# Hybrid sparse/differential attention layers: projection chunks by row block in two banks, and side steps regrouped

## The reference

```python
h = _rmsnorm(x, pre_norm_g[i]); z = h @ w_in[i]
qa, ka, va, qi, ki, wi, ga, qb, kb, vb, gb = _split_in(z)      # rope on q, k of all groups
# group A: an indexer scores the keys, each query keeps its 64 best admissible ones
iscore = sum_h relu(qi_h . ki / 8) * wi_h
oa = softmax(qa . ka / 8 over the kept keys) @ va              # 8 heads of 64
# group B: differential attention, block-causal in chunks of 64
attn = softmax(q1 . k1 / 8) - lam * softmax(q2 . k2 / 8)       # 4 heads, 2 maps each
ob = _rmsnorm(attn @ vb, subln_g[i]) * (1 - lam_init)
y = concat([oa * silu(ga), ob * silu(gb)]) @ w_out[i]
x = x + _rmsnorm(y, post_norm_g[i])
e = (p[i] @ w_ple_proj[i]) * sigmoid(x @ w_ple_gate[i])
x = x + _rmsnorm(e, ple_norm_g[i])
```

## Time and profile before

| | us |
|---|---|
| median of 3 runs | 362.15 (361.76 to 362.46) |
| profiled execution, its own time | 362.61 |
| span of its trace | 360.8 |
| PE busy | 351.3 |
| DVE, ACT, POOL busy | 264.8, 226.9, 68.1 |

### The profile page before, as it was taken

One profiled execution on the slowest core, in us unless ns is written; L12 is line 12 of the kernel. 1 busy time (PEld: TensorE's weight loads), 2 busy tenths in 40 slices (PEclk: granted clock), 3 DMA queues, 4 the chain that ended last, 5 costly groups with the idle time before them and its releaser, 6 DMA issues.

```text
span 360.8 us, 5644 instructions
## 1 busy us (share of the span) xinstructions
PE 351.3 (97%) x1901; PEld 290.0 (80%) x1901; DVE 264.8 (73%) x560; ACT 226.9 (63%) x459; POOL 68.1 (19%) x121
## 2 busy tenths in 40 slices
PE   7999999999999999999999999999999999999992
PEld 6897887888888888888888888778888878888881
DVE  2884977989966676786786587888996658678543
ACT  3985476686678764655665565778576786365221
POOL 1144173061500000003105315004250000000000
PEclk9999999999999999999999999999999999999999
DMA  7994378763764455657575828347458337550011
GB/s 253 380 358 133 105 228 150 258 184 109 201 212 128 161 180 171 184 171 154 187 216 161 255 74 236 109 124 219 127 160 239 127 118 233 173 162 17 0 51 67
DMA packets 31948, 61.12 MB, mean 169 GB/s; under 512 B 2376, under 2 KB 4688, under 8 KB 31920
## 3 DMA queue, kind: packets, MB, share of 16 engines
q1 hardware_dynamic: 30784, 57.48, 50.6%
q0 software_dynamic: 1120, 3.28, 4.5%
q10 hardware_dynamic: 16, 0.00, 0.0%
HBM read 59.71 MB, written 1.05 MB: 168 GB/s over the span
## 4 chain that ended last, share of the span: by engine, by line
PE 92%; issue 2%; DMA 2%; DVE 1%; ACT 1%; SPq 0%; POOL 0%; POOLq 0%; DVEq 0%
PE proj L1157 26%; PE proj L1159 25%; PE proj L1158 25%; PE sc L1298 3%; PE sc L1240 3%; PE tr L1311 2%; DMA resid<-in_x_dram 2%; PE tr L1258 2%; PE pv L1332 2%; PE pv L1327 1%; PE proj L1118 1%; PE proj L1097 1%; PE proj L1109 1%; PE sc L1189 1%; PE sc L1269 0%
## 5 line engine op out<-in xcount | busy, mean ns | idle before, releaser
L1157 PE MATMUL proj<-w_hi,act_hi 128*128 128x512 f32 (+1 forms) x400 | 160.8, 402 | 0.0
L1159 PE MATMUL proj<-w_hi,act_lo 128*128 128x512 f32 (+1 forms) x400 | 155.3, 388 | 0.0
L1158 PE MATMUL proj<-w_lo,act_hi 128*128 128x512 f32 (+1 forms) x400 | 154.9, 387 | 0.0
L798 DVE TENSOR_TENSOR w_lo<-raw,w_hi 128x1024 fp32r<-128x1024 f32 (+1 forms) x102 | 122.0, 1210 | 20.7 <-ACT w_hi L581 19.7
L581 ACT ACTIVATE w_hi<-raw 128x1024 fp32r<-128x1024 f32 (+2 forms) x103 | 103.3, 1025 | 4.5 <-DMA raw<-in_w_ple_proj_dram 2.1
L1159 PEld LDWEIGHTS proj<-w_hi,act_lo 128*128 128x128 f32 x400 | 75.1, 188 | 15.9
L1157 PEld LDWEIGHTS proj<-w_hi,act_hi 128*128 128x128 f32 x400 | 75.2, 188 | 15.4 <-issue 0.7
L1158 PEld LDWEIGHTS proj<-w_lo,act_hi 128*128 128x128 f32 x400 | 75.3, 188 | 13.0
L522 POOL TENSOR_TENSOR rstd<-var,minus_half 128x1 f32<-128x1 f32 x12 | 6.8, 564 | 182.6 <-DVE var L788 160.6
L699 ACT ACTIVATE probs<-probs,neg_max 128x128 f32<-128x128 f32 (+1 forms) x64 | 28.2, 445 | 1.9 <-DVE neg_max L941 1.9
L581 ACT ACTIVATE pT<-tr 128x512 f32<-128x512 f32 (+1 forms) x22 | 12.7, 576 | 16.3 <-PE tr L1311 11.0
(11 more groups left out here) (179 smaller groups left out, 410.4 us busy)
## 6 DMA issues: line engine op xcount, KB each, us to landing
raw<-in_w_in_dram SPq DMA_DIRECT2D x59, 512.0 KB, 4.4
raw<-in_w_out_dram SPq DMA_DIRECT2D x16, 512.0 KB, 3.4
raw<-in_w_ple_gate_dram SPq DMA_DIRECT2D x16, 512.0 KB, 3.9
raw<-in_w_in_dram SPq DMA_DIRECT2D x7, 324.0 KB, 5.0
raw<-in_w_ple_proj_dram SPq DMA_DIRECT2D x4, 512.0 KB, 3.6
resid<-in_x_dram SPq DMA_DIRECT2D x2, 512.0 KB, 8.0
probs<-in_w_in_dram SPq DMA_DIRECT2D x2, 512.0 KB, 9.3
g_ple<-in_ple_norm_g_dram POOLq DMA_DIRECT2D x2, 512.0 KB, 7.1
```

Of the source, the lines that this page charges most:

```text
L798: nc.vector.tensor_tensor(w_lo[:, g % SLOTS, 0:nk * cols], landing(g, nk * cols), w_hi[:, g % SLOTS, 0:nk * cols].bitcast(fp32), ALU.subtr ...
L1157: nc.tensor.matmul(ps, src_hi[:, b, k0 + k, :], hi, start=(first_u and k == 0), stop=False)
L1158: nc.tensor.matmul(ps, src_hi[:, b, k0 + k, :], lo, start=False, stop=False)
L1159: last = nc.tensor.matmul(ps, src_lo[:, b, k0 + k, :], hi, start=False, stop=last_k)
```

## The change

1. The pieces of the middle chunks run by row block: four of block 0, then four of block 1. All chunks but QB now use the banks `proj0` (block 0) and `proj1` (block 1). `wait_bank` is rewritten for it: GA's block b now waits for `glu_done` of GB's block b.
2. S2 is issued right behind S1, at place 15, and S5 right behind S4, at 42, on TensorE alone; they go to `proj2` and `proj3`. VectorE reads them at the old steps S2 (18) and S5 (44).
3. PV3 moves from 43 to 42 and there stands behind the logits; PV4 moves from 50 to 52, ahead of PV5. PT8 goes to `kT` and does not wait for a value product.
4. The sigmoid and product of GB's row block 0 become a step of their own, `glu`, at place 46.
5. Other places: S3, E3 one earlier, S4, E4 one later, PT3 and PT4 one earlier, PT5 and PT6 one later, T KA 0 at 32.

The core of the diff:

```diff
-    KA=[33, 37],
-    S=[12, 15, 18, 35, 41, 43],
-    E=[13, 16, 24, 37, 42, 44],
+    KA=[32, 37],
+    S=[12, 15, 18, 34, 42, 44],
+    E=[13, 16, 24, 36, 43, 44],
-    PT=[19, 23, 26, 41, 42, 44, 45, 50, 51],
-    PV=[20, 25, 28, 43, 50, 52],
+    PT=[19, 23, 26, 40, 41, 45, 46, 50, 51],
+    PV=[20, 25, 28, 42, 52, 52],
+    glu=46,
+S_WITH = {1: 2, 4: 5}
-        mms(chunk, both, dict(enumerate(mid[c * len(both):(c + 1) * len(both)])))
+        mms(chunk, one(0) + one(1), dict(enumerate(mid[c * len(both):(c + 1) * len(both)])))
-            return 2 * (IN_CHUNKS.index(chunk) % 2) + b
+            return 2 + b if chunk == "QB" else b
...
+        def s_bank(i):
+            return proj[2 + i % 2] if i // 2 in S_WITH.values() else sc[i % 2]
+        def pt_slot(n):
+            return kT[:, :, :] if n == 8 else pT[:, n % 3, :, :]
...
+                elif kind == "glu":
+                    wait_sum(act, L, "GB", 0, s[1])
+                    gate_sigmoid(L, "GB", s[1])
...
                 elif chunk == "GA":
-                    pe.wait_ge(v_out, L * 4 + 2 + b + 1)
+                    pe.wait_ge(glu_done, L * 4 + b + 1)
+                elif chunk == "WO" and b == 0:
+                    pe.wait_ge(max_done, L * 12 + 12)
...
-                elif kind == "S":
+                elif kind == "S" and s[1] not in S_WITH.values():
...
+                    logits(L, s[1], g, b, keys)
+                    if s[1] == 1:
+                        pe.wait_ge(z_out, L * 8 + 2)
+                        logits(L, 2, g, b, keys)
+                    elif s[1] == 4:
+                        pe.wait_ge(max_done, L * 12 + 6)
+                        logits(L, 5, g, b, keys)
```

More of the change, by code:

```diff
@@ L594, in emb_copy, with gate_sigmoid @@
                 copy(emb[:, b, n * N:(n + 1) * N], proj[bank_of("PLE", n, b, L)][:, :]).then_inc(ple_out, 1)
+            def gate_sigmoid(L, chunk, b):
+                if chunk == "GA":
+                    act.wait_ge(y_done, L * 2 + b + 1)
+                elif L > 0:
+                    act.wait_ge(t8_done, (L - 1) * 12 + t8_index("y", b, 0) + 1)
+                nc.scalar.activation(gate[:, b, :], proj[bank_of(chunk, 0, b)][:, :], ACT.Sigmoid).then_inc(sig_done, 1)
             act.dma_start(g8[:, :], pre_norm_g[0, :].rearrange("(k p) -> k p", p=P)).then_inc(g8_in, 16)
@@ L633, in _ @@
                     else:
[L634 to L639, removed]
+                        gate_sigmoid(L, chunk, b)
+                elif kind == "glu":
+                    wait_sum(act, L, "GB", 0, s[1])
+                    gate_sigmoid(L, "GB", s[1])
                 elif kind == "pT":
@@ L801, in _ @@
                 kind = s[0]
[L802 to L805, removed]
+                if kind in ("mm", "glu"):
+                    chunk, n = UNITS[s[1]][:2] if kind == "mm" else ("GB", 0)
+                    b = s[-1]
+                    if kind == "mm" and (s[1] != LAST_OF[chunk, n] or chunk not in ("GA", "GB") or (chunk, b) == ("GB", 0)):
                         continue
@@ L1110, in rest_part, with logits @@
                                      w_hi[:, u, k * cols:(k + 1) * cols], start=False, stop=False)
+            def logits(L, n, g, b, keys):
+                for j in range(N // keys):
+                    for part in range(1 if b == 0 else 3):
+                        for odd in range(2):
+                            m = s_task(2 * n + odd)[2][j]
+                            rows = slice(odd * HEAD, (odd + 1) * HEAD)
+                            if b == 0:
+                                q, k = qT[g][rows, m // 2, 0:P], kT[rows, m // 2, :]
+                            else:
+                                q = (q_lo if part == 2 else q_hi)[rows, m // 2, :]
+                                k = (k_lo if part == 1 else k_hi)[rows, m // 2, :]
+                            end = part == (0 if b == 0 else 2)
+                            ins = nc.tensor.matmul(s_bank(2 * n + odd)[:, j * keys:(j + 1) * keys], q, k,
+                                                   start=(part == 0), stop=end)
+                            if end and j == N // keys - 1:
+                                ins.then_inc(s_done, 1)
             def low_part(u, b, src_hi):
@@ L1284, in _ @@
                     else:
[L1285 to L1290, removed]
-                                rows = slice(odd * HEAD, (odd + 1) * HEAD)
-                                if b == 0:
-                                    q, k = qT[g][rows, m // 2, 0:P], kT[rows, m // 2, :]
-                                else:
-                                    q = (q_lo if part == 2 else q_hi)[rows, m // 2, :]
-                                    k = (k_lo if part == 1 else k_hi)[rows, m // 2, :]
-                                end = part == (0 if b == 0 else 2)
-                                ins = nc.tensor.matmul(sc[odd][:, j * keys:(j + 1) * keys], q, k, start=(part == 0),
-                                                       stop=end)
-                                if end and j == n_maps - 1:
-                                    ins.then_inc(s_done, 1)
+                        pe.wait_ge(max_done, L * 12 + {1: 2, 3: 4, 4: 8}[s[1]])
+                    logits(L, s[1], g, b, keys)
[5 more added lines that the diff above has]
+                        logits(L, 5, g, b, keys)
                 elif kind == "PT":
@@ L1326, in _ @@
                         if g == 0:
-                            last = nc.tensor.matmul(pv[:, h * P:(h + 1) * P], pT[:, n % 3, j, :],
+                            last = nc.tensor.matmul(pv[:, h * P:(h + 1) * P], pt_slot(n)[:, j, :],
                                                     v_all[:, kt, 0, h * P:(h + 1) * P], start=(kt == 0),
```

29 lines of the change are left out of this document (14 added, 15 removed).

## The result

The changed kernel takes **366.48 us** (median of 5 runs, 365.40 to 367.18) against 362.15 before (5 runs, 361.76 to 362.46). The ratio is 1.0106, with a 95% interval of 1.0090 to 1.0122: slower by 1.1%. The forecast was 365.8, within 363.5 to 368.5.

A forecast was written before the change was run, and what follows sets the result against it. The prediction took TensorE's queued work as the bound, busy 351.3 of 360.8 us. Per layer +2.44 - 0.44 - 0.17 = +1.83, +3.66 for two, on 362.61 gives 366.27, as a median 365.8 (range 363.5 to 368.5).

The forecast's parts named there:

- The chain to piece 48: From PV3 through ScalarE's exponentials and sigmoid to VectorE's product of GB: GA's first piece starts 2.44 us later per layer.
- the drain of 1.38: At ScalarE's table load before the sigmoid: by the skill page, 1.4 us longer wait per layer, sum 368.6; not adopted.
- Part 1: Logits S1 and S2 in one TensorE visit: 0.44 us saved per layer.
- Part 2: S4, S5 and PV3 in one visit: pieces 40 to 47 take 15.61 against 16.03, 0.42 us saved per layer without waits.
- Part 3: PV4 and PV5 together at place 52: 0.17 us saved per layer.
- behind another one it adds 1.01: Value product directly behind another in one visit: costs 1.01 us, where PV4 alone costs 1.18.
- The restart: TensorE resuming after its waits before GA's first piece: 0.15 us beyond the wait, with 0 and 0.3 as ends.
- The sum: Per layer +2.44 - 0.44 - 0.17 = +1.83 us; +3.66 for two layers.
- The signs: Trace marks expected: two waits per layer, E4 behind qT_a, 24 logits in a row, TensorE busy about 2 us less.
- The wait was there: Rival at GA's first piece: no wait there, so only savings stand, 360.1 us; 11 in 100, partial waits included.
- No further waits: Rival around places 16 to 25: more waits on ScalarE and VectorE, 368.2 us; 11 in 100 for over 1 us.
- The clock did not fall: Rival behind the new wait: TensorE's clock drops to 1.2 GHz for two pieces, 2.7 us per layer, 371.2; 4 in 100.

The follow-up runs named there:

- e1: Changed kernel with GA in banks proj2 and proj3, so its first piece no longer waits for GB's product; 362.46 us, ratio 0.9991.
- e2: Changed kernel with E4 ahead of PV3's copy on ScalarE and S5's maxima one place earlier, at 43; 364.53 us, ratio 1.0046.
- e6: Kernel before, with GA's first matmul of block 0 also waiting for VectorE's product of GB's block 0; 369.83 us, ratio 1.0188.
- e4: Kernel e3 with S2 moved back to place 18 and the sc banks, in a visit of its own; 361.38 us, ratio 0.9968.
- e3: Changed kernel with GA in proj2 and proj3 and E4 ahead of PV3's copy; 359.99 us, ratio 0.9914; repeated on another chip 360.91 us, ratio 0.9949.
- e5: Kernel e4 with PV4 also moved back to place 50; 361.72 us, ratio 0.9992.
- e10: Changed kernel with the transposes PT6 moved from place 46 to 48, behind GA's first piece; 369.43 us, ratio 1.0191.

## Why the prediction was right, and where its terms were off

**The chain to piece 48: right, nearly row by row.** All times of the profile after are 0.21 later (piece 40 starts at 103.48 and not 103.27: an opening 0.70 longer, less 0.48 saved). With that taken off:

| step | predicted | measured, less 0.21 |
|---|---|---|
| PV3 starts | 109.98 | 110.00 |
| its copy `qT_a` | 111.12 | 111.14 |
| E4 starts | 112.54 | 112.58 |
| sigmoid starts | 120.27 | 120.31 |
| product of GB ends | 121.59 | 121.63 |
| piece 48 starts | 121.74 | 121.69 |

The wait came in two parts as worked out, 0.84 and 1.54 for "about 1.0" and "about 1.7". The term was +2.44 per layer and measured +2.38. e1 and e2 show by taking them away that these were its two causes, and e6 that the wait gives the same 18.4 with nothing else changed.

The trace shows no drain around the table load: it starts at 119.23 and lasts 1.28, and the sigmoid starts at 120.52, 0.01 behind. By the drain of 1.38 that the Trainium skill gives (ScalarE: Activation LUTs, "What ACT_TABLE_LOAD costs") the sum was 368.6; the runs gave 366.48, and the measurement decides.

**Part 1 (S1 and S2): right,** 0.44 predicted, 0.48 in the changed kernel, 0.43 to 0.46 by e4.

**Part 2 (S4, S5, PV3): right as to the visit, too large as to the stretch, and without effect on this result.** I worked out 15.61 for pieces 40 to 48 if nobody waits; e3 shows 15.80, so 0.24 saved and not 0.42. The visit behind piece 42 is nearly as predicted: pieces 42 and 43 with it take 4.20 + 1.51 = 5.71 in e3, for 1.37 + 2.85 + 1.37 = 5.59, and 0.09 of the 0.12 is the slower first matmul behind PT4's transposes, which is in their 0.45 already. Most of the 0.19 lies at PT5 and PT6. Pieces 45 to 47 with their two transposing visits take 1.72 + 1.96 + 1.47 = 5.15, for 3 x 1.37 + 2 x 0.45 = 5.01. The transposes of PT6 are the place: `tr` is freed by PT5's copy (115.62, 0.59 long) and they start right behind it.

```profile
115.94 0.40 PE L1193 MATMUL proj<-w_hi,act_lo 128*128 128x512 f32 x1
116.26 0.66 PE L1335 MATMUL tr<-ident,probs 128*128 128x128 f32 x4
```

That is a wait of about 0.1, which stands in no list of waits. In the changed kernel the whole term can't be seen: piece 48 starts when ScalarE's chain ends, whatever TensorE has saved after PV3. I had counted it in the same way ("not 0.42 earlier").

**Part 3 (PV4 and PV5): right in sign, half the size.** 0.17 predicted, 0.33 measured by e5. The failed step is "behind another one it adds 1.01". That figure came from PV3 behind a row of projections and ahead of logits, which is another neighbourhood. Between two value products nothing else stands, as the rows of both show:

```profile
126.42 1.53 PE L1356 MATMUL pv<-pT,v_all 128*64 128x128 f32 x24
127.78 0.61 PE L1356 MATMUL pv<-kT,v_all 128*64 128x128 f32 x8
```

Piece 52 with its side steps lasts 3.87 in e3, for 3.00 before with one product less: the second one costs 0.87. The first one alone costs 1.17 (piece 50 lasts 2.89 with it and 1.72 without), as predicted (1.18). That the difference is the change of form is my reading, here and in Part 1. The runs show what a visit costs alone and behind another; they don't separate the form from the rest of going in and out, and four transposes, whose form is that of the pieces, also make the first matmul behind them 0.09 slower. In the changed kernel 48 to 56 shows only 0.18 less, since piece 48 restarts there 0.13 slower (1.49 for 1.36).

**The restart: 0.15 taken, about 0.2 measured** (0.06 from the end of the product to piece 48, and 0.13 inside it).

**The sum.** +1.83 per layer predicted, +1.72 in the trace. 3.44 for both layers on the median of before gives 365.6, and the median measured is 0.9 above it. In the profiled run 0.70 of that is a longer opening. The other four runs have no trace, so where the 0.9 lies in them stays open; the interval of the ratio, 3.3 to 4.4 us, has room for 3.44.

**The signs.** Most came as written: both waits twice (1.54 and 0.84), E4 behind `qT_a`, 24 logits in a row, 18.4 between pieces 40 and 48, a clock of 1.00 behind the wait. One was wrong: TensorE's busy sum fell by 0.3 and not by about 2. The busy time of the middle pieces fell by 0.68 and 0.64 per layer and not by 1.03: in pieces 40 to 48 it is 16.03 as before, because the modelled ends of the matmuls ahead of the two waits count as busy and hide what Part 2 saved. The opening of the profile has 0.98 us more busy time.

**The rivals.** The wait was there. No further waits came: pieces 0 to 40 are shorter by exactly the saving. The clock did not fall, but here the forecast had luck. I had looked at the length of the parts beside the last idle stretch; e6 and e10 show that an unbroken stretch of 2.2 to 3.1 us can be enough, and that the same kernel without PT6 between its two waits did lose 2.8 us in one layer. 4 in 100 was too little for this rival. The Trainium skill's rule (TensorE: Matmul & The Clock Gate, "Why this matters for your kernels") that gaps without work take the clock down is borne out in layer 0 of e10 and not in its layer 1, behind an equal gap; e6 shows a fall with a gap of 2.19 us, which is shorter than those that the page warns of.

## What to carry to other kernels

When a change gives a buffer a new and earlier use, follow the chain that frees it from its first event on, row by row on the engine that does the work, also where that chain never mattered before: here it ended 2.6 us after TensorE could have used the bank, and nobody had waited for it. An idle gap on the other engine just ahead of the chain is a place to put work into, not slack: moving the exponentials into it was worth 0.9 us per layer, a free pair of banks 1.7, and the two together turned a kernel 1.1% slower into one 0.5 to 0.9% faster. Putting matmuls of equal form into one visit saves going in and out once more, 0.3 to 0.5 us per visit here, but only if TensorE is what the end waits for. And if a wait in mid-kernel can't be avoided, work put into the middle of it is worth a try: here the clock stayed up in four of four cases with it, and fell in three of four without.

## What the runs showed of the hardware that I had not expected

- One unbroken idle stretch of TensorE of 2.19 us (both layers of e6) or 3.06 us (layer 0 of e10) came with a granted clock of 0.50, the level of 1.2 GHz: in e6 for 3.4 us (123.3 to 126.7), from 0.9 us behind the restart at 122.40 on, and in e10 for 6.8 us (120.6 to 127.4), from 0.8 us ahead of the restart at 121.37 on. The price was 1.7 and 2.8 us beyond the wait. The same 3.06 us in layer 1 of e10 had no such effect. Stretches of 0.84 and 1.54, or 0.90 and 1.01, with work between, had none.
- 32 value products in a row (two sets of 16) cost 0.87 us for the second set, where one set alone in a visit costs 1.17. Logits in a row cost 0.12 per pair, 0.7 for twelve, where twelve alone cost 1.14.
